# A recurrence's chunk solver on one NeuronCore: two heads or two chunks in one fp32 matmul, with orders on VectorE and ScalarE and three bulk loads moved around it

## The chip, the cores and the metric

One core of one Trainium2 chip. The metric is device time in microseconds for one execution of the whole program, as the median of several runs.

## The reference, cut to what matters

Two blocks of two layers each act on a sequence of 256 positions of 1024 features, all in fp32. Most of the work is the large products of the feed-forward layers. The change lies in one mixer, an RWKV-7 layer with 16 heads of 64 features:

```python
def step(state, inp):
    r_t, w_t, k_t, v_t, a_t, b_t = inp
    sa = jnp.einsum('bhij,bhj->bhi', state, a_t)
    state = (state * w_t[:, :, None, :] + sa[..., None] * b_t[:, :, None, :]
             + v_t[..., None] * k_t[:, :, None, :])
    y_t = jnp.einsum('bhij,bhj->bhi', state, r_t)
    return state, y_t
```

The kernel doesn't step through 256 positions. It takes chunks of 64 positions, and solves each chunk's 64 by 64 triangular system for every head by repeated doubling.

## The kernel before, in words

Weights stream from DRAM in units of 128x1024 through a ring of 6 (`RING`). ScalarE makes each unit's high part (`split_hi`), VectorE its low part (`split_lo`), up to 4 units (`AHEAD`) before TensorE uses it, and three fp32r products give fp32 accuracy. Every engine runs one fixed list of instructions; they meet at semaphores (`wait_ge`, `then_inc`).

`rwkv_in_stage` makes r, k, v and the decays. It goes through 24 units (`m` is the unit's number), with the elementwise work hung between the splits. At m = 19 and m = 21 TensorE turns tiles of them (`R.turn`, 16 transposes each), and `R.turn_out` copies the results out, even jobs on ScalarE (L1741), odd ones on VectorE (L1743). The turn at m = 19 waits for r times the decay (`R_MADE`, L2119). At its end SyncE issues the load of `g2` (L1875), and the Head's `sync` those of two rows of gains, `ln0` and `ln1` (L2612, L2614).

`solve_stage` then runs twice, for t = 0 and t = 1 (128 positions, so two chunks each), with `step_stage` behind each. It has a first part (`gram_low`, `gram_two`: products of 64x64 blocks, masked by VectorE in L2378, L2382 and L2385, while GpSimd masks in L2367), five levels (`LEVELS`), and a last part (L2303, L2308). The 16 heads are in two halves of 8 (`half`), 4 pairs (`q`) of 2 (`e`). At each level and half TensorE does

- `first_product` (L2221), called P1 here: 32 matmuls, one for each head and chunk, each with 64 rows and 64 columns of weights and 32 columns of data, so that each lies in one quadrant of the array;
- `turned` (L2228), called T: 4 transposes of 128x128;
- after both halves' P1 and T, `second_product` (L2238), called P2, of half 0 and half 1, 32 matmuls each;
- `with_values` (L2209), called V here, once a level except at the last: 32 matmuls of 64x64x64 whose results ScalarE takes out in `copy_values` (L2322).

P2 of a half waits for ScalarE's copies of P1 (L2335) and T (L2339), and for t = 0 also for VectorE's copy of one half of T (L2393). P1 of the next level waits for VectorE's addition of P2's result (`m_made`, L2400, two instructions a half, one for each `e`) and for GpSimd's mask (L2367). At levels 1 and 3 P1 of half 0 also waits for V's own end (`kv_bank`). The last part waits for the last level's `m_made`. For t = 1 the Head hangs its VectorE work in between (`while_solving`), and one long ScalarE activation (`head.square`, L2638) at level 2. 

Of the kernel before, what the change touches and what calls it, by code (L numbers as in the profile page):

```python
# [12 lines left out]
P = 128  # L13
# [185 lines left out]
def unit_done(c, eng, n):  # L199
    eng.wait_ge(c.unit_used, n + 1)  # L200
# [1597 lines left out]
def rwkv_in_stage(c, join, mu_col, recurrence):  # L1798
# [52 lines left out]
    def sync(sp):  # L1851
# [5 lines left out]
        for m in range(count):  # L1857
# [4 lines left out]
            if m == 12:  # L1862
# [10 lines left out]
                sp.dma_start(c.work[:, 19, 512:768], c.dram["smask"][:, :]).then_inc(s["rows"].sem, 16)  # L1873
        unit_done(c, sp, first + count - 1)
        sp.dma_start(c.recur[:, 3, :], c.dram["g2"][:, :]).then_inc(c.g2_in.sem, 16)  # L1875

# [170 lines left out]
    def vector(dve):  # L2047
# [15 lines left out]
        for n in range(BEFORE, AHEAD):  # L2063
            c.split_lo(dve, first + n)
        for m in range(count):
            c.split_lo(dve, first + AHEAD + m)
            if m == 0:
# [45 lines left out]
            if m == 16:  # L2113
                dve.wait_ge(*at("mix_rows", 64))
                nc.vector.scalar_tensor_tensor(wexc, kk, -1.0, wexc, ALU.mult, ALU.mult)
            if m == 17:
                unit_done(c, dve, first + 15)
                for q in range(4):
                    last = nc.vector.tensor_tensor(quad(r, q), quad(r, q), c.bank[4 + q][:, :], ALU.mult)  # L2119
                last.then_inc(s["value"].sem, 1)  # L2120
            if m == 18:
                dve.wait_ge(*at("value", R_MADE))
                nc.vector.tensor_tensor(tmp, r, k, ALU.mult).then_inc(s["value"].sem, 1)
            if m == 19:
                dve.wait_ge(*at("rows", ALL_ROWS))
                dve.wait_ge(*at("value", RK))
                order.link(dve, nc.vector.tensor_tensor(tmp, tmp, rk_row, ALU.mult))
            if m in (20, 22):
                for j in (1, 3):
                    R.turn_out(c, dve, j + 2 * (m - 20))  # L2130
            if m == 21:
# [5 lines left out]
def solve_stage(c, R, head):  # L2137
# [12 lines left out]
              "m_bank": N * LEVELS, "m_made": N * LEVELS, "final": N}  # L2150
    s = c.marks("mix_", counts)
    chunks = [slice(CHUNK * ch, CHUNK * (ch + 1)) for ch in range(2)]
    head_rows = [slice(HD * e, HD * (e + 1)) for e in range(2)]
# [63 lines left out]
    def first_product(level, half):  # L2217
        X = R.solver[half]
        for q, e, ch in quarters(((0, 0), (1, 1), (1, 0), (0, 1))):
            cols, tok = slice((2 * q + e) * CHUNK, (2 * q + e + 1) * CHUNK), chunks[ch]  # L2220
            last = nc.tensor.matmul(p_bank[half][ch][head_rows[e], q * HC:(q + 1) * HC], X.low_part[tok, cols],  # L2221
                                    right_columns(X.m[tok, cols], level), start=True, stop=True)
        last.then_inc(s["p1_bank"].sem, 1)
# [8 lines left out]
    def second_product(half):  # L2232
        X = R.solver[half]
        for q, e, ch in quarters(((0, 0), (1, 1), (0, 1), (1, 0))):
            rows, tok = head_rows[e], chunks[ch]
            left = X.t[rows, q * P + ch * CHUNK:q * P + (ch + 1) * CHUNK]
            right = X.p1[rows, ch * P + q * HC:ch * P + (q + 1) * HC]
            last = nc.tensor.matmul(m_bank[half][e][tok, q * HC:(q + 1) * HC], left, right, start=True, stop=True)  # L2238
        last.then_inc(s["m_bank"].sem, 1)
# [92 lines left out]
    def copy_products(act, level, half):  # L2332
        step, X = level * N + half, R.solver[half]
        act.wait_ge(*at("p1_bank", step + 1))
        nc.scalar.activation(X.p1[:, 0:S].rearrange("p (c n) -> p c n", c=2), p_both[half][:, :, 0:P],  # L2335
                             ACT.Copy).then_inc(s["p1_made"].sem, 1)
        act.wait_ge(*at("t_bank", step + 1))
        for i in range(1 + t):
            last = nc.scalar.activation(t_part(half, i), t_in(half, i), ACT.Copy)  # L2339
        last.then_inc(s["t_act"].sem, 1)  # L2340

    def scalar(act):
# [4 lines left out]
        for level in range(LEVELS):  # L2347
            for half in range(N):
                copy_products(act, level, half)
                if level and (level - 1) % N == half:  # L2350
                    copy_values(act, level - 1)
                if t == 1 and level == 2 and half == 0:
                    head.square(act, 0)
        for half in range(N):
# [18 lines left out]
    def vector(dve):  # L2373
# [14 lines left out]
        for level in range(LEVELS):  # L2388
# [5 lines left out]
            for half in range(N):  # L2394
                step, X = level * N + half, R.solver[half]
                dve.wait_ge(*at("m_bank", step + 1))
                for e in range(2):
                    m = pairs(X.m)[:, :, e, :].rearrange("p q (g s b) -> p q g s b", s=2, b=2 << level)[:, :, :, 1, :]
                    new = m_bank[half][e][:, 0:P].rearrange("p (q g b) -> p q g b", q=4, b=2 << level)
                    last = nc.vector.tensor_tensor(m, m, new, ALU.add)  # L2400
                last.then_inc(s["m_made"].sem, 1)
# [173 lines left out]
class Head:  # L2575
# [33 lines left out]
    def sync(self, sp):  # L2609
        c = self.c  # L2610
        sp.wait_ge(c.bonus_made.sem, c.bonus_made.at(1))
        sp.dma_start(self.ln0, c.dram["rrows"][3, :, :]).then_inc(c.g2_in.sem, 16)  # L2612
        sp.wait_ge(c.step_state.sem, c.step_state.at(2))
        sp.dma_start(self.ln1, c.dram["rrows"][4, :, :]).then_inc(self.rows.sem, 16)  # L2614

# [763 lines left out]
```

## Time and profile before

| | |
|---|---|
| median of 3 runs | 2150.77 us (2149.77 to 2151.74) |
| the profiled execution's own time | 2150.07 us |
| its span | 2148.3 us |
| TensorE, busy share of the span | 98% |
| VectorE, ScalarE, GpSimd | 71%, 53%, 17% |
| the recurrence, from the first gram product to the next stage's first product | about 1801 to 1898 us |

The span runs from the first to the last instruction of the program. Busy TensorE time contains pipelined matmuls, so it is not time at peak. A matmul's duration in the trace is its latency (0.22 us for the small ones), and several run at once; what a group costs is the distance from its start to the next group's start.

### The profile page before, as it was taken

Reading aid. Unit: us, or ns where it says so; the run is one execution under the profiler, and the core shown is the slowest. Engines: PE = TensorE matmul, PEld = TensorE weight load, DVE = VectorE, ACT = ScalarE, POOL = GpSimd, SP = SyncE. Lnnn points to the kernel's source line nnn. Section 1 sums busy time; section 2 is a strip of 40 time slices with the busy share of each in tenths; the row PEclk is TensorE's granted clock in tenths of the full one; section 3 lists DMA queues with packets and bytes.
Section 4 is the critical chain, followed back from the end, with each engine's and each line's share of the span. In section 5 each row is a group of like instructions: output and inputs, shape, how many; then the busy total and the mean of one; then the engine's idle time right before and its main releaser. Section 6 shows DMA issues by size and latency. Waiting matters only on the chain.

```text
span 2148.3 us, 39019 instructions
## 1 busy us (share of the span) xinstructions
PE 2111.2 (98%) x13570; PEld 1799.1 (84%) x13570; DVE 1515.4 (71%) x2383; ACT 1146.8 (53%) x1953; POOL 367.1 (17%) x462
## 2 busy tenths in 40 slices
PE   8999999999999999999999999999999999899998
PEld 7888888888888788888888988888888787768887
DVE  6666976667667966667667757667766797677666
ACT  5455755446446754555446446446545564355455
POOL 1111211112111211112111002111111212301111
PEclk9999999999999999999999999999999999999999
DMA  7655435555656345546556555565555452035553
GB/s 253 199 181 185 146 120 201 197 189 174 202 179 194 117 149 194 195 166 206 195 182 228 188 177 166 184 195 205 203 201 180 151 185 94 14 109 200 199 180 131
DMA packets 104401, 376.70 MB, mean 175 GB/s; under 512 B 11764, under 2 KB 12276, under 8 KB 104180
## 3 DMA queue, kind: packets, MB, share of 16 engines
q1 hardware_dynamic: 104308, 375.42, 52.2%
q8 instruction: 63, 1.03, 0.2%
q14 instruction: 30, 0.25, 0.0%
HBM read 373.29 MB, written 1.05 MB: 174 GB/s over the span
## 4 chain that ended last, share of the span: by engine, by line
PE 87%; DVE 7%; ACT 4%; issue 1%; POOL 1%; DMA 1%; SPq 0%; DVEq 0%; POOLq 0%; ACTq 0%
PE bank L951 27%; PE bank L955 14%; PE bank L190 13%; PE bank L191 13%; PE bank L192 13%; DVE w_lo L184 2%; ACT act L480 1%; PE bank L1234 1%; DVE act L591 1%; ACT w_hi L177 0%; PE bank L2238 0%; PE bank L2228 0%; PE bank L2221 0%; PE bank L390 0%; DVE x L576 0%
## 5 line engine op out<-in xcount | busy, mean ns | idle before, releaser
L951 PE MATMUL bank<-act,w_hi 128*128 128x512 f32 x2816 | 704.3, 392 | 2.6 <-DVE act L591 1.5
L951 PEld LDWEIGHTS bank<-act,w_hi 128*128 128x128 f32 x2816 | 514.7, 188 | 106.0 <-DVE act L591 4.2
L804 DVE TENSOR_TENSOR w_lo<-raw,w_hi 128x1024 fp32r<-128x1024 f32 x432 | 502.8, 1219 | 4.3 <-issue 1.0
L795 ACT ACTIVATE w_hi<-raw 128x1024 fp32r<-128x1024 f32 x432 | 424.9, 1050 | 2.3
L955 PEld LDWEIGHTS bank<-act,w_lo 128*128 128x128 f32 x2816 | 384.0, 190 | 27.7
L955 PE MATMUL bank<-act,w_lo 128*128 128x256 f32 x2816 | 392.5, 282 | 0.0
L904 DVE TENSOR_TENSOR work<-bank,work 128x256 f32<-128x256 f32 x176 | 74.7, 425 | 376.4 <-ACT work L825 376.4
L184 DVE TENSOR_TENSOR w_lo<-raw,w_hi 128x1024 fp32r<-128x1024 f32 x248 | 294.6, 1219 | 52.5 <-ACT w_hi L177 52.1
L865 POOL TENSOR_TENSOR work<-work,rb 128x256 f32<-128x256 f32 x176 | 130.0, 739 | 1035.2 <-DVE work L898 1033.5
L190 PE MATMUL bank<-w_hi,g_hi 128*128 128x512 f32 x704 | 277.3, 394 | 1.0 <-DVE w_lo L184 0.9
L191 PE MATMUL bank<-w_lo,g_hi 128*128 128x512 f32 x704 | 275.9, 392 | 0.0
L192 PE MATMUL bank<-w_hi,g_lo 128*128 128x512 f32 x704 | 274.0, 389 | 0.0
L177 ACT ACTIVATE w_hi<-raw 128x1024 fp32r<-128x1024 f32 x248 | 250.7, 1051 | 42.0 <-PE bank L192 34.8
L815 ACT ACTIVATE work<-bank 128x256 f32<-128x256 f32 x176 | 67.3, 382 | 304.7 <-PE bank L955 304.2
L820 ACT ACTIVATE work<-work 128x256 f32<-128x256 f32 x176 | 73.5, 418 | 285.2 <-POOL work L865 285.0
L190 PE MATMUL bank<-w_hi,act 128*128 128x512 f32 x496 | 197.8, 399 | 2.5 <-DVE act L2761 1.4
L192 PE MATMUL bank<-w_hi,act 128*128 128x512 f32 x496 | 193.3, 390 | 0.0
L191 PE MATMUL bank<-w_lo,act 128*128 128x512 f32 x496 | 193.3, 390 | 0.0
L192 PEld LDWEIGHTS bank<-w_hi,g_lo 128*128 128x128 f32 x704 | 132.2, 188 | 28.9
L190 PEld LDWEIGHTS bank<-w_hi,g_hi 128*128 128x128 f32 x704 | 132.8, 189 | 26.0 <-DVE w_lo L184 2.6
L191 PEld LDWEIGHTS bank<-w_lo,g_hi 128*128 128x128 f32 x704 | 132.8, 189 | 21.1
L870 POOL TENSOR_TENSOR work<-work,rb 128x256 f32<-128x256 f32 x176 | 130.2, 740 | 91.6 <-ACT work L820 91.6
(291 smaller groups left out, 2210.4 us busy)
## 6 DMA issues: line engine op xcount, KB each, us to landing
raw<-w_dram SPq DMA_DIRECT2D x680, 512.0 KB, 4.4
work<-rows_dram SPq DMA_DIRECT2D x13, 512.0 KB, 6.3
work<-rrows_dram SPq DMA_DIRECT2D x5, 512.0 KB, 4.5
x<-x_dram SPq DMA_DIRECT2D x2, 512.0 KB, 3.8
out<-x SPq DMA_DIRECT2D x4, 256.0 KB, 2.0
work<-work SPq DMA_DIRECT2D x2, 504.0 KB
work<-g_dram SPq DMA_DIRECT2D x1, 640.0 KB, 10.1
work<-dist_dram SPq DMA_DIRECT2D x2, 256.0 KB, 5.0
```

The source lines that it names most:

```text
L177: self.nc.scalar.activation(self.w_hi[:, n % RING, :], self.raw[:, n % RING, :], ACT.Copy).then_inc(self.hi_ready, 1)
L184: self.nc.vector.tensor_tensor(self.w_lo[:, n % RING, :], self.raw[:, n % RING, :], self.w_hi[:, n % RING, :].bitcast(F32), ALU.subtract). ...
L190: nc.tensor.matmul(out, stat_hi, mov_hi, start=first, stop=False)
L191: nc.tensor.matmul(out, stat_hi, mov_lo, start=False, stop=False)
L192: return nc.tensor.matmul(out, stat_lo, mov_hi, start=False, stop=last)
L795: nc.scalar.activation(c.w_hi[:, n % RING, :], c.raw[:, n % RING, :], ACT.Copy).then_inc(c.hi_ready, 1)
L804: nc.vector.tensor_tensor(c.w_lo[:, n % RING, :], c.raw[:, n % RING, :], c.w_hi[:, n % RING, :].bitcast(F32), ALU.subtract).then_inc(c.lo_ ...
L865: nc.gpsimd.tensor_tensor(c.gate_scaled[:, t % 2, :], c.gate_sum[:, t % 2, :], c.rb[:, :], ALU.mult).then_inc(s["gate_scaled"].sem, 1)
L870: nc.gpsimd.tensor_tensor(c.silu_scaled[:, t % 2, :], c.silu[:, t % 2, :], c.rb[:, :], ALU.mult).then_inc(s["silu_scaled"].sem, 1)
L904: nc.vector.tensor_tensor(c.up_sum[:, p, :], up[p][:, 0:S], c.up_sum[:, p, :], ALU.add).then_inc(s["product"].sem, 1)
L951: nc.tensor.matmul(bank[:, :], c.w_hi[:, slot(m), k * P:(k + 1) * P], c.act[:, k, :, :], start=k == 0, stop=False)
L955: return nc.tensor.matmul(bank[:, 0:S], c.w_lo[:, slot(m), k * P:(k + 1) * P], c.act_hi[:, k, :], start=False, stop=k == KT - 1)
```

## The change

P1 takes both heads of a pair as 128 columns of weights: 8 matmuls with 64 rows, 128 columns and 64 columns of data in place of 32. Half of what comes out (head e's weights with head e's data is wanted, the crossed blocks are not) is left unread. P2 takes both chunks as 128 columns of weights in the same way: 8 matmuls in place of 32. So ScalarE copies P1 out in two instructions of 64 partitions each (one for each head of the pairs), and VectorE adds P2 in four instructions a half, each over 64 partitions. `copy_values` and `head.square` come after both halves' copies of a level. In `rwkv_in_stage` VectorE's product for r comes ahead of unit 17's split, jobs 1 and 3 are copied out at m = 19 instead of 20, and the product with `rk_row` is at m = 20 instead of 19. The loads of g2 and ln0 wait for the first P1 of t = 0, that of ln1 also for the first P1 of t = 1.

```diff
@@ rwkv_in_stage, sync
-        unit_done(c, sp, first + count - 1)
-        sp.dma_start(c.recur[:, 3, :], c.dram["g2"][:, :]).then_inc(c.g2_in.sem, 16)
@@ rwkv_in_stage, vector
         for m in range(count):
+            if m == 17:
+                unit_done(c, dve, first + 15)
+                for q in range(4):
+                    last = nc.vector.tensor_tensor(quad(r, q), quad(r, q), c.bank[4 + q][:, :], ALU.mult)
+                last.then_inc(s["value"].sem, 1)
             c.split_lo(dve, first + AHEAD + m)
...
-            if m == 17:
...
             if m == 19:
+                for j in (1, 3):
+                    R.turn_out(c, dve, j)
+            if m == 20:
                 dve.wait_ge(*at("rows", ALL_ROWS))
                 dve.wait_ge(*at("value", RK))
                 order.link(dve, nc.vector.tensor_tensor(tmp, tmp, rk_row, ALU.mult))
-            if m in (20, 22):
-                for j in (1, 3):
-                    R.turn_out(c, dve, j + 2 * (m - 20))
+            if m == 22:
+                for j in (5, 7):
+                    R.turn_out(c, dve, j)
@@ solve_stage
     def first_product(level, half):
         X = R.solver[half]
-        for q, e, ch in quarters(((0, 0), (1, 1), (1, 0), (0, 1))):
-            cols, tok = slice((2 * q + e) * CHUNK, (2 * q + e + 1) * CHUNK), chunks[ch]
-            last = nc.tensor.matmul(p_bank[half][ch][head_rows[e], q * HC:(q + 1) * HC], X.low_part[tok, cols],
-                                    right_columns(X.m[tok, cols], level), start=True, stop=True)
+        for q in range(4):
+            cols = slice(q * P, (q + 1) * P)
+            for ch, tok in enumerate(chunks):
+                last = nc.tensor.matmul(p_bank[half][ch][:, q * CHUNK:(q + 1) * CHUNK], X.low_part[tok, cols],
+                                        right_columns(X.m[tok, cols], level), start=True, stop=True)
...
     def second_product(half):
         X = R.solver[half]
-        for q, e, ch in quarters(((0, 0), (1, 1), (0, 1), (1, 0))):
-            rows, tok = head_rows[e], chunks[ch]
-            left = X.t[rows, q * P + ch * CHUNK:q * P + (ch + 1) * CHUNK]
-            right = X.p1[rows, ch * P + q * HC:ch * P + (q + 1) * HC]
-            last = nc.tensor.matmul(m_bank[half][e][tok, q * HC:(q + 1) * HC], left, right, start=True, stop=True)
+        for q in range(4):
+            for e, rows in enumerate(head_rows):
+                right = X.p1[rows, 0:S].rearrange("p (c q n) -> p c q n", c=2, n=HC)[:, :, q, :]
+                last = nc.tensor.matmul(m_bank[half][e][:, q * CHUNK:(q + 1) * CHUNK], X.t[rows, q * P:(q + 1) * P],
+                                        right, start=True, stop=True)
...
     def copy_products(act, level, half):
-        nc.scalar.activation(X.p1[:, 0:S].rearrange("p (c n) -> p c n", c=2), p_both[half][:, :, 0:P],
-                             ACT.Copy).then_inc(s["p1_made"].sem, 1)
+        for e, rows in enumerate(head_rows):
+            own = p_both[half][rows, :, 0:S].rearrange("p c (q e n) -> p c q e n", e=2, n=HC)[:, :, :, e, :]
+            last = nc.scalar.activation(X.p1[rows, 0:S].rearrange("p (c q n) -> p c q n", c=2, n=HC), own, ACT.Copy)
+        last.then_inc(s["p1_made"].sem, 1)
...
             for half in range(N):
                 copy_products(act, level, half)
-                if level and (level - 1) % N == half:
-                    copy_values(act, level - 1)
-                if t == 1 and level == 2 and half == 0:
-                    head.square(act, 0)
+            if level:
+                copy_values(act, level - 1)
+            if t == 1 and level == 2:
+                head.square(act, 0)
...
                 for e in range(2):
-                    new = m_bank[half][e][:, 0:P].rearrange("p (q g b) -> p q g b", q=4, b=2 << level)
-                    last = nc.vector.tensor_tensor(m, m, new, ALU.add)
+                    new = m_bank[half][e][:, 0:S].rearrange("p (q c g b) -> p q c g b", q=4, c=2, b=2 << level)
+                    for ch, tok in enumerate(chunks):
+                        last = nc.vector.tensor_tensor(m[tok], m[tok], new[tok, :, ch, :, :], ALU.add)
@@ Head.sync
+        grams_over = [recurrence.first_product for recurrence in self.R]
+        sp.wait_ge(grams_over[0].sem, grams_over[0].at(1))
+        sp.dma_start(c.recur[:, 3, :], c.dram["g2"][:, :]).then_inc(c.g2_in.sem, 16)
         sp.wait_ge(c.bonus_made.sem, c.bonus_made.at(1))
         sp.dma_start(self.ln0, c.dram["rrows"][3, :, :]).then_inc(c.g2_in.sem, 16)
         sp.wait_ge(c.step_state.sem, c.step_state.at(2))
+        sp.wait_ge(grams_over[1].sem, grams_over[1].at(1))
         sp.dma_start(self.ln1, c.dram["rrows"][4, :, :]).then_inc(self.rows.sem, 16)
```

On VectorE, from the split of unit 17 to the end of `rwkv_in_stage`, the order before (L184 is a split, L2119 the product for r, L2123 r times k, L2127 the product with `rk_row`, L1743 a copy of turned tiles, L2132 the sum for the bonus):

```order
L2115 SCALAR_TENSOR_TENSOR work<-work 128x2048
L184 TENSOR_TENSOR w_lo<-raw,w_hi 128x1024
L2119 TENSOR_TENSOR work<-work,bank 128x512 x4
L184 TENSOR_TENSOR w_lo<-raw,w_hi 128x1024
L2123 TENSOR_TENSOR work<-work 128x2048
L184 TENSOR_TENSOR w_lo<-raw,w_hi 128x1024
L2127 TENSOR_TENSOR work<-work 128x2048
L184 TENSOR_TENSOR w_lo<-raw,w_hi 128x1024
L1743 COPY recur<-bank 128x512 x2
```

and of the change (L2118 is the old L2115, L2067 the old L2119, L2121 the old L2123, L2128 the old L2127):

```order
L2118 SCALAR_TENSOR_TENSOR work<-work 128x2048
L2067 TENSOR_TENSOR work<-work,bank 128x512 x4
L184 TENSOR_TENSOR w_lo<-raw,w_hi 128x1024 x2
L2121 TENSOR_TENSOR work<-work 128x2048
L184 TENSOR_TENSOR w_lo<-raw,w_hi 128x1024
L1743 COPY recur<-bank 128x512 x2
L184 TENSOR_TENSOR w_lo<-raw,w_hi 128x1024
L2128 TENSOR_TENSOR work<-work 128x2048
```

The product for r is one split earlier, and the first two copies come before the product with `rk_row`; the copies of jobs 5 and 7 keep their place.

On ScalarE, levels 1 and 2 of the solver for t = 1, before (L2335 copies P1, L2339 T, L2322 V's result, L2638 is the Head's square):

```order
L2335 ACTIVATE work<-bank 128x256
L2339 ACTIVATE work<-bank 128x2x128 x2
L2322 ACTIVATE work<-bank 128x512
L2335 ACTIVATE work<-bank 128x256
L2339 ACTIVATE work<-bank 128x2x128 x2
L2335 ACTIVATE work<-bank 128x256
L2339 ACTIVATE work<-bank 128x2x128 x2
L2638 ACTIVATE recur<-work 128x1024
L2335 ACTIVATE work<-bank 128x256
L2339 ACTIVATE work<-bank 128x2x128 x2
L2322 ACTIVATE work<-bank 128x512
```

and of the change (L2340, L2344, L2325 and L2648 in their places):

```order
L2340 ACTIVATE work<-bank 64x256 x2
L2344 ACTIVATE work<-bank 128x2x128 x2
L2340 ACTIVATE work<-bank 64x256 x2
L2344 ACTIVATE work<-bank 128x2x128 x2
L2325 ACTIVATE work<-bank 128x512
L2340 ACTIVATE work<-bank 64x256 x2
L2344 ACTIVATE work<-bank 128x2x128 x2
L2340 ACTIVATE work<-bank 64x256 x2
L2344 ACTIVATE work<-bank 128x2x128 x2
L2325 ACTIVATE work<-bank 128x512
L2648 ACTIVATE recur<-work 128x1024
```

The copies of half 1 no longer stand behind V's copy or the square.

## Rows read from the trace of the kernel before

**Rows 1.** The page's first part: busy time, share of the span, instructions.
```profile
PE 2111.2 (98%) x13570; PEld 1799.1 (84%) x13570; DVE 1515.4 (71%) x2383; ACT 1146.8 (53%) x1953; POOL 367.1 (17%) x462
```
**Rows 2.** Window, t = 1's levels: length; busy PE, PEld, DVE, ACT, POOL; clock; DMA; GB/s.
```profile
1857.00:1880.00 23.00, 19.90 (x703) 17.13 (x701) 14.45 (x27) 10.78 (x29) 12.91 (x7) 1.00 0.02 4
```
**Rows 3.** Timeline of TensorE, two other stages: start us, length us, line, weights, data, count.
```profile
283.92 1.05 PE L1249 MATMUL bank<-const,work 128*128 128x1 f32 x8
...
247.90 1.14 PE L1200 MATMUL bank<-work 64*128 64x256 f32 x8
```
**Rows 4.** Groups by line and shape, P1: count, busy us, mean ns, idle before.
```profile
L2221 PE MATMUL bank<-work 64*64 64x32 f32 x640 | 15.1, 221 | 3.0 <-issue 1.5 <-DVE work L2382 0.9
```
**Rows 5.** Timeline of TensorE, levels 1 to 4 of t = 0, to the last part's first matmul.
```profile
1812.31 1.04 PE L2221 MATMUL bank<-work 64*64 64x32 f32 x32
...
1822.06 0.67 PE L2221 MATMUL bank<-work 64*64 64x32 f32 x32
...
1823.24 0.67 PE L2221 MATMUL bank<-work 64*64 64x32 f32 x32
1823.84 0.66 PE L2228 MATMUL bank<-const,work 128*128 128x128 f32 x4
1824.43 1.35 PE L2238 MATMUL bank<-work 64*64 64x32 f32 x64
1825.57 1.10 PE L2209 MATMUL bank<-work 64*64 64x64 f32 x30
1826.45 0.25 PE L2221 MATMUL bank<-work 64*64 64x32 f32 x2
...
1830.72 0.69 PE L2303 MATMUL bank<-work 64*64 64x64 f32 x32
```
**Rows 6.** VectorE and ScalarE: copies of T in both solvers, an addition of P2's result.
```profile
1824.54 0.42 DVE L2393 COPY work<-bank 128x256 f32<-128x256 f32 x1 [0.76 <-PE bank L2228]
1830.09 0.48 DVE L2400 TENSOR_TENSOR work<-work,bank 128x128 f32<-128x128 f32 x2 [0.20 <-PE bank L2238]
...
1877.43 0.66 ACT L2339 ACTIVATE work<-bank 128x256 f32<-128x256 f32 x2 [0.17 <-PE bank L2228]
```
**Rows 7.** Timeline of TensorE, t = 1, with the idle time ahead in brackets.
```profile
1848.37 2.30 PE L2196 MATMUL bank<-recur 64*64 64x128 f32 x75 [0.95 <-issue]
...
1857.65 0.30 PE L2221 MATMUL bank<-work 64*64 64x32 f32 x4
...
1876.13 0.67 PE L2221 MATMUL bank<-work 64*64 64x32 f32 x32
...
1878.23 1.06 PE L2238 MATMUL bank<-work 64*64 64x32 f32 x32 [0.24 <-ACT work L2339]
1879.11 0.69 PE L2303 MATMUL bank<-work 64*64 64x64 f32 x32
...
1882.55 0.27 PE L2308 MATMUL bank<-work 64*64 64x64 f32 x2 [0.54 <-issue]
```
**Rows 8.** Waits from 1800 to 1900 us: in total, times, longest.
```profile
PE bank L2238 <- ACT work L2339: 1.7, 5, 0.6
...
PE bank L2221 <- issue: 1.5, 4, 0.5
```
**Rows 9.** Timelines at the head: TensorE's turn and first gram product, VectorE's last copies.
```profile
1785.46 1.94 PE L1731 MATMUL bank<-const,work 128*128 128x128 f32 x16 [1.05 <-DVE work L2119]
...
1800.87 0.69 PE L2189 MATMUL bank<-recur 64*64 64x64 f32 x32
...
1798.82 1.28 DVE L1743 COPY recur<-bank 128x512 f32<-128x512 f32 x2
```
**Rows 10.** VectorE's mask L2382 for t = 0 and t = 1, and GpSimd's two masks beside it.
```profile
1803.83 0.69 DVE L2382 TENSOR_TENSOR work<-work,const 128x512 f32<-128x512 f32 x1
...
1847.73 1.69 DVE L2382 TENSOR_TENSOR work<-work,const 128x512 f32<-128x512 f32 x1
...
1802.69 2.97 POOL L2367 TENSOR_TENSOR work<-work,const 128x512 f32<-128x512 f32 x2 [30.34 <-ACT work L2315]
```

More of the change, by code:

```diff
@@ L2115, in vector @@
                 nc.vector.scalar_tensor_tensor(wexc, kk, -1.0, wexc, ALU.mult, ALU.mult)
-            if m == 17:
[L2117 to L2120, printed above, removed]
             if m == 18:
@@ L2151, in solve_stage @@
     s = c.marks("mix_", counts)
+    R.first_product = s["p1_bank"]
     chunks = [slice(CHUNK * ch, CHUNK * (ch + 1)) for ch in range(2)]
```

## The prediction

> **What bounds the kernel.** I read the page first: TensorE is busy 98% of the span [rows 1], so outside the recurrence the kernel is a stream of matmuls that this change leaves alone. What can move lies between about 1782 and 1898 us. Next I read the window of t = 1's levels: the granted clock is 1.00 (2.4 GHz), no engine but TensorE is near full, and even TensorE has only 19.9 us busy in 23 [rows 2]. Then the timeline of TensorE through the levels, group by group [rows 5, 7], because busy time of overlapping small matmuls says little; the waits tell what ended its gaps [rows 8]. The reader should see a chain there: P1 and T of half 0, P1 and T of half 1, copies of T, P2 of half 1, V, next level. TensorE waits for ScalarE 5 times, 1.7 us in all, and P1's matmuls alone were held back 1.5 us by "issue", that is by no semaphore [rows 8]; these sit inside groups and are waits for instructions, as I read them.
>
> **P1 and P2 on TensorE.** Today P1 has 32 matmuls in 0.60 us from its start to T's (1823.24 to 1823.84) [rows 5], 8 in each quadrant. A P1 matmul lasts 221 ns [rows 4], so some 0.38 of the 0.60 us is issue and the rest is the end of the last one, which T needs since it uses the whole array. In the change 8 matmuls lie in two row groups, 4 in each. What do 4 cost? With 128 columns of weights and a single column of data the pitch is (1.05 - 0.25) / 7 = 0.114 us (L1249) [rows 3], so such a matmul is paced by its weights, and 64 columns of data hide behind them. Two row groups run side by side: 8 matmuls of 64x128 with 256 columns take 1.14 us, where one after another would be twice that (L1200) [rows 3]. So 4 x 0.114, less what the first doesn't wait for, is 0.40 us to the last start, and 0.15 for its end: 0.55 us. **A quarter of the matmuls, but 0.05 us less for a group.** A P2 goes the same way: 0.40 in place of the 0.57 that the pair's 1.14 us give it (1824.43 to 1825.57) [rows 5]. But V behind it works in 64x64, and P1 behind V in 64x128. I charge 0.14 us for each such change of shape, as P1 to T has it (0.15 above), so P2 of half 1 to V is 0.54 and V to P1 is 0.88 + 0.13 = 1.01 us (1825.57 to 1826.45) [rows 5], or about 1.27 where P1 waits for V's end (levels 1 and 3; 1.24 today).
>
> No row here has 64x64 next to 64x128, so nothing may be lost there; that is the lower end, 12 x 0.13 = 1.6 us better. The Trainium skill, TensorEngine Tiling (Array Packing), Key Properties, says that changing the tiling mode drains TensorE, which speaks for the charge and against the change. By that rule my sum stands; without it the sum would be 1.6 us lower.
>
> **The chain through the copies.** Let y be the start of half 1's P1. T of half 1 starts at y + 0.55. In t = 0 VectorE's copy starts 0.70 after T does and takes 0.42 (1823.84, 1824.54) [rows 5, 6], and P2 starts 0.12 later: y + 1.79 in place of y + 1.84. In t = 1 ScalarE has two copies, 0.66, starting 0.70 after T, and P2 follows at 1878.23, 0.14 after 1878.09 [rows 6, 7]: y + 2.05 in place of the 2.10 of level 4 (1876.13 to 1878.23). The second copy of P1 costs ScalarE 0.28 us more (0.66 for two against 0.385 for one), and hides: P1's copies start at y + 0.70 and leave the engine free at y + 1.26, when T is there. So faster matmuls alone bring 0.05 us a half.
>
> **The longer addition.** Two additions take 0.48 us (1830.09) [rows 6], so the pitch is 0.20 and four take 0.89. They bear on the path once in each solver, at its end: the last part's first matmul waits for half 0's addition. That was 1.36 after P2's start, and becomes 0.70 + 0.89 + 0.15 = 1.74. Elsewhere half 0's addition ends by y + 2.87, while V keeps TensorE until y + 3.3, and that cover is 0.45 us in t = 0 and 0.7 in t = 1. The 64 partitions I take at the price of 128.
>
> **Sum for t = 0**, levels 1 to 4: the blocks are 0.55 + 0.58 + 1.79 + 0.54 + 1.01 = 4.47; with the wait 4.73; 4.47; and last 0.55 + 0.58 + 1.14 + 1.74 = 4.01. That is 17.7 against 1830.72 - 1812.31 = 18.4 [rows 5]: **-0.7 us**, all of it from stalls such as that of level 1's P1, which takes 1.04 in place of 0.67. Level 0 doesn't change.
>
> **Sum for t = 1**: 0.55 + 0.58 + 2.05 + 0.54 + 1.01 = 4.73; 4.99; 4.73; 4.01; in all 18.5 against 1879.11 - 1857.65 = 21.5 [rows 7]: -3.0, less 0.1 at level 0: **-2.9 us**. Two things make it: 1.45 us of P1's stalls go (1920 of TensorE's instructions fewer in the two solvers, a matmul and a load of weights for each of 960), and half 1's copies no longer stand behind copy_values and the square, of the 1.7 us of waits the larger part. The square moved by 2 us still ends before VectorE has added half 1 of level 2 and asks for it.
>
> **The loads.** g2 and ln0 (1 MB) land during t = 0's first levels instead of its gram products, ln1 5 us later than before. Their readers come much later (gain row and gate in t = 1), so the delay costs nothing. With ln1 away from t = 1's gram products I expect the stall of 0.95 us there [rows 7] to go. But VectorE is the longer there, its L2382 taking 1.69 us [rows 10], so TensorE's gain is hidden, but for an earlier P1: GpSimd's next mask is then out of the way of VectorE's second L2382. **-0.4**, between 0 and -0.6. The stall of 0.54 in the last part [rows 7] should go with the others, as the queue is ahead: **-0.4**.
>
> **VectorE in rwkv_in_stage.** The turn at m = 19 waits 1.05 us for the product for r [rows 9]; a split earlier it is there 1.1 us sooner, and TensorE reaches the gram product at 1799.8 or sooner. But job 7 must be out first, and VectorE, which is full here with the same work in another order, copies it until 1800.10 [rows 9]. So the gram starts at 1800.2 in place of 1800.87: -0.7. Against it: GpSimd's masks come 1 us sooner with ScalarE, VectorE's first L2382 0.7 us sooner. In t = 0 it slipped between GpSimd's two masks (0.69), in t = 1 it met the second one and took 1.69 [rows 10]. I expect t = 0 to meet it too, +1.0, and half of that back at the second L2382. **-0.2**, between -0.7 and +0.3.
>
> **Sum**: -0.2 - 0.7 - 0.4 - 2.9 - 0.4 = -4.6 us, from the profiled execution's 2150.07 (span 2148.3) to 2145.5. The median of the runs is 0.7 above that execution, so the forecast is **2146.2**. A measurement of this kernel tells about 0.2%, 4.3 us, from no change; the forecast is just past it.
>
> **The rivals.**
> *Instructions go on stalling* (chance 0.22). The stalls may follow the fetching of blocks and not how many instructions are used, or come back elsewhere. For it: V and the gram products, as dense as before, remain, and the bulk loads now lie beside the levels. Against it: t = 0's gram products ran without a stall beside a bulk load. Then about 1.45 + 0.7 + 0.4 of the gain is lost, nearly 2.7 with the hidden 0.1: 2148.9.
> *No charge for a change of shape* (0.17): 1.6 us lower, 2144.6.
> *The matmuls are paced by their number* (0.04). At 0.60 / 32 = 19 ns each, 8 would take 0.15. That shortens each P1 and P2 by a further 0.25 on the path, three groups in each of 8 levels, 6 us: 2140. L1249's pitch speaks against it.
> *Slower: the clock falls* (0.03). The granted clock is 1.00 with TensorE 87% busy [rows 2]; the change issues a quarter of the P1 and P2 matmuls. If that took the clock to 1.2 GHz in the levels of t = 1, groups worth about 3.5 us a level would double, 4 x 3.5 = 14 us: 2160. It decides from the first window where the clock reads under 1; two levels of it outweigh the gain. Nothing in the rows is near it.
> *VectorE and GpSimd meet badly in both solvers*, or the added copies don't hide (0.04): 1.5 to 2 us lost, 2148.
>
> **The numbers.** My forecast has 0.50, and of its spread of about 1 us 0.6 lies past 0.2%. Faster: 0.30 + 0.17 + 0.04 = 0.51. Within 0.2%: 0.20 + 0.22 + 0.04 = 0.46. Slower 0.03. The range reaches from the second rival less 1 us to the first plus 0.6 us: 2143.5 to 2149.5.
>
> **What would show it.** P1 to T 0.55 us with 8 matmuls; P2 of half 1 to V 0.54; in t = 1 P2 of half 1 at P1 + 2.05 in each level; levels of 4.5 us in t = 0 and 4.8 in t = 1; no "issue" gap over 0.2 us in the solvers; the first gram product at 1800.2; the addition 0.89. A P1 group under 0.4 us, a V that follows P2 at once, or gaps by "issue" of the old size would each prove a step wrong.

## The result, and the profile after

The change takes 2161.57 us (2161.27 to 2162.39), the kernel before, beside it on the same chip, 2151.26 us (2149.77 to 2153.04). The ratio is 1.0051, with an interval of 1.004 to 1.0061: **slower by 10.3 us**. The forecast was 2146.2, its range ended at 2149.5, and slower by over 0.2% had a chance of 0.03. The profiled execution took 2161.52 us, its span 2159.7.

The page's first part, which answers to [rows 1]:

```profile
PE 2128.1 (99%) x12930; PEld 1816.4 (84%) x12930; DVE 1531.4 (71%) x2423; ACT 1155.1 (53%) x1973; POOL 366.9 (17%) x462
```

TensorE has 640 matmuls fewer than before, 13570 less 12930. The prediction took 960. The groups by line and shape, 1780 to 1912 us, show why (count, busy us, mean ns, idle before); P1 is L2224, P2 L2240:

```profile
L2224 PE MATMUL bank<-work 64*128 64x64 f32 x320 | 22.2, 277 | 0.8 <-PE bank L2211 0.6
L2240 PE MATMUL bank<-work 64*128 64x64 f32 x320 | 21.0, 276 | 0.1
```

In 20 groups (5 levels, 2 halves, 2 solvers) 320 is 16 a group, not 8. **One fp32 matmul call of the code is two matmuls in the trace**, and two loads of weights. Before, P1 calls 16 matmuls a group (4 pairs, 2 heads, 2 chunks) and the trace has 32; the change calls 8 and the trace has 16. The text ahead set the code's 8 beside the trace's 32. The number is halved, not quartered.

The timeline of TensorE through level 2 of t = 0, where before has [rows 5], and the end of the levels (start, length, line, weights, data, count, idle time before in brackets):

```profile
1819.35 1.11 PE L2224 MATMUL bank<-work 64*128 64x64 f32 x16
1820.39 0.66 PE L2231 MATMUL bank<-const,work 128*128 128x128 f32 x4
1820.98 1.11 PE L2224 MATMUL bank<-work 64*128 64x64 f32 x16
...
1822.61 2.00 PE L2240 MATMUL bank<-work 64*128 64x64 f32 x32
1824.54 1.15 PE L2211 MATMUL bank<-work 64*64 64x64 f32 x32
1825.85 1.11 PE L2224 MATMUL bank<-work 64*128 64x64 f32 x16 [0.16 <-PE bank L2211]
...
1835.36 2.00 PE L2240 MATMUL bank<-work 64*128 64x64 f32 x32
1837.84 0.69 PE L2306 MATMUL bank<-work 64*64 64x64 f32 x32 [0.48 <-DVE work L2406]
```

P1 to T is 1.04 us (1819.35 to 1820.39), 0.60 before and 0.55 predicted. The two P2 take 1.93 to V (1822.61 to 1824.54), 1.14 before. The level is made of TensorE alone: twice P1 to T (1.04) and T to the next group (0.59), the two P2 (1.93) and V to P1 (1.31) are 6.50 us; 0.16 of it is a wait for V's end. Before, levels 1 to 3 of t = 0 took 4.7 us each on average, from P1's start to the next P1's.

The starts of the single matmuls in the same trace say how they lie. In the change's P1 they start in pairs, the two of a pair 7 ns apart, and behind the first pair a new one starts every 0.112 us. Before, P1's start in fours, again 7 ns apart, and behind the first four new ones start every 0.058 us. So two matmuls with 128 columns of weights lie side by side, and four with 64 columns do.

Windows of the levels of t = 0 and t = 1 (length; busy PE, PEld, DVE, ACT, POOL; clock; DMA; GB/s):

```profile
1812.00:1831.00 19.00, 18.68 (x312) 16.81 (x308) 9.18 (x30) 8.31 (x21) 7.64 (x6) 1.00 0.01 2
1857.00:1880.00 23.00, 22.38 (x340) 19.35 (x337) 19.25 (x38) 11.17 (x29) 10.20 (x7) 1.00 0.08 25
```

In t = 1 TensorE is busy 22.4 us of 23 with 340 matmuls, against 19.9 with 703 in [rows 2]. Neither ScalarE nor VectorE holds it up for long: in t = 1 a level takes 6.49 us where the same level of t = 0 takes 6.26, because the second half's P2 starts some 0.2 us later, behind ScalarE's copies: the two P2 take 2.16 us to V there (1874.60 to 1876.76), in place of 1.93. The granted clock is 1.00 in both: it isn't the cause.

Two more lines, of TensorE at the first gram product and at the last part of t = 1, and of VectorE:

```profile
1799.85 0.69 PE L2191 MATMUL bank<-recur 64*64 64x64 f32 x32 [1.31 <-DVE recur L1743]
...
1894.21 0.27 PE L2311 MATMUL bank<-work 64*64 64x64 f32 x2 [1.02 <-issue]
```
```profile
1802.80 1.69 DVE L2387 TENSOR_TENSOR work<-work,const 128x512 f32<-128x512 f32 x1
...
1836.51 2.39 DVE L2406 TENSOR_TENSOR work<-work,bank 64x128 f32<-64x128 f32 x8 [0.62 <-PE bank L2240]
```

Where the time went, start of the change less start of before: the gram product of t = 0 comes 1.0 us earlier (1799.85, 1800.87), the last part of t = 0 7.1 us later (1837.84, 1830.72), the last part of t = 1 11.2 later (1890.30, 1879.11). The stage behind and the end of the span have 11.4 to 11.7. So 8.1 us are lost between the first gram product and the last part of t = 0, 4.1 between there and the last part of t = 1, and 0.5 in the last part's longer stall (1.02 in place of 0.54). Nearly all of it is in the two solvers' levels: levels 1 to 4 take 24.7 and 25.5 us, where before has 18.4 and 21.5.

### The profile page after: what moved, and what is told of

It is laid out like the page before. It is cut to its first block, busy times and chain, and to the rows that moved or that the text cites. A ratio compares the mean times of both kernels' runs of the same rounds, so it can differ in the third digit from the quotient of the medians.

```text
span 2159.7 us, 37800 instructions
## 1 busy us (share of the span) xinstructions
PE 2128.1 (99%) x12930; PEld 1816.4 (84%) x12930; DVE 1531.4 (71%) x2423; ACT 1155.1 (53%) x1973; POOL 366.9 (17%) x462
## 4 chain that ended last, share of the span: by engine, by line
PE 87%; DVE 7%; ACT 3%; issue 2%; POOL 1%; DMA 1%; SPq 0%; DVEq 0%; POOLq 0%; ACTq 0%
PE bank L951 27%; PE bank L955 14%; PE bank L190 13%; PE bank L191 12%; PE bank L192 12%; DVE w_lo L184 2%; PE bank L2224 1%; PE bank L2240 1%; ACT act L480 1%; PE bank L1234 1%; ACT w_hi L177 1%; DVE act L591 1%; PE bank L2231 0%; PE bank L390 0%; DVE x L576 0%
## 5 line engine op out<-in xcount | busy, mean ns | idle before, releaser
L184 DVE TENSOR_TENSOR w_lo<-raw,w_hi 128x1024 fp32r<-128x1024 f32 x248 | 294.6, 1220 | 52.0 <-ACT w_hi L177 51.6
```

The lines of the kernel that those rows point to most:

```text
L184: self.nc.vector.tensor_tensor(self.w_lo[:, n % RING, :], self.raw[:, n % RING, :], self.w_hi[:, n % RING, :].bitcast(F32), ALU.subtract). ...
```

## The experiments

The theory after the result: **pairs load 128 columns for each matmul and lie in two row groups, so half the matmuls take longer than all of them in four quadrants.** Rivals: the copies and additions over 64 partitions; the new orders and loads. Each time below stands beside a kernel before of its own, measured along with it, and the ratio is to that one; those of the runs below lie between 2150.8 and 2152.1 us.

**a1: the orders and loads without the new products.** P1, P2, their copies and additions are those of before.

```diff
-                last = nc.tensor.matmul(p_bank[half][ch][:, q * CHUNK:(q + 1) * CHUNK], X.low_part[tok, cols], ...
+            last = nc.tensor.matmul(p_bank[half][ch][head_rows[e], q * HC:(q + 1) * HC], X.low_part[tok, cols], ...
```

> The change without its new products: P1 and P2, their copies and additions as before; only the orders on VectorE and ScalarE and the three moved loads remain. If the new groups of TensorE are what costs (P1 start to T 1.04 us after, 0.60 before), this is faster than before: the gram product starts about 1 us sooner, half 1's P2 in t = 1 loses its waits behind V's copy and the square (about 1 us), so 2147 to 2150 us. If the orders or the loads are what costs, it is as slow as the change, 2158 us or more.

2151.85 us, ratio 0.9999 (0.999 to 1.0009). That misses the 2147 to 2150, and it is nowhere near 2158. Taken together the orders and loads bring nothing and cost nothing; the loss is in the products and what hangs on them. In a1's trace the two solvers differ. In t = 1, with ScalarE's new order, levels 1 to 4 take 20.0 us, before 21.5. In t = 0 they take 21.7, before 18.4. There the gain goes into a stall and the half clock behind it, as TensorE's timeline and a window of a1 show:

```profile
1826.84 0.64 PE L2223 MATMUL bank<-work 64*64 64x32 f32 x28
1828.89 0.30 PE L2223 MATMUL bank<-work 64*64 64x32 f32 x2 [1.42 <-issue]
```
```profile
1830.00:1837.00 7.00, 7.00 (x199) 6.60 (x194) 2.32 (x7) 2.11 (x6) 0.00 (x0) 0.52 0.02 5
```

Inside a P1, TensorE waited 1.42 us for nothing that the profile shows; 1 us later the granted clock was at half (1.2 GHz) for 6.8 us. That is one execution, a slow one among a1's ten (2152.97 us).

**a2: the same results in quadrants.** The banks, the split copies and the additions are the change's; P1 and P2 go back to one head and one chunk a matmul.

```diff
-        for q in range(4):
-            cols = slice(q * P, (q + 1) * P)
-            for ch, tok in enumerate(chunks):
-                last = nc.tensor.matmul(p_bank[half][ch][:, ...], X.low_part[tok, cols], ...
+        for q, e, ch in quarters(((0, 0), (1, 1), (1, 0), (0, 1))):
+            last = nc.tensor.matmul(p_bank[half][ch][head_rows[e], ...], X.low_part[tok, own], ...
```

> The change with its wide products cut into quadrants: each matmul has 64 columns of weights and 64 of data, the same results in the same places, twice the number of matmuls, and the split copies and additions stay. Theory 'weights' (a matmul with 128 columns of weights is paced by loading them, 0.111 us each, and only two run side by side): P1 to T goes back to 0.60 us though the number of matmuls doubles and each still moves 64 columns, levels to 4.5 to 5 us, time 2147 to 2152. Rival 'splits' (two copies and four additions are what costs): P1 may shorten but the time stays above 2157. Rival 'data' (64 columns of data in place of 32 are what costs): P1 stays near 1.0 us.

2154.58 us, ratio 1.0013 (1.0004 to 1.0023). Its TensorE:

```profile
1817.93 0.69 PE L2223 MATMUL bank<-work 64*64 64x64 f32 x32
1818.55 0.66 PE L2230 MATMUL bank<-const,work 128*128 128x128 f32 x4
```

P1 has 32 matmuls with the change's 64 columns of data and takes 0.62 us to T, against 1.04. Against its own before a2 is 2.8 us slower where the change is 10.3, so with the same results in the same places 7.5 us are gone. The time misses the 2147 to 2152 as well as the rival's 2157. What stays lies in t = 1: its levels 1 to 4 take 23.8 us, where a1 has 20.0, and TensorE waits there 2.3 us in five for ScalarE's copies and 1.4 us once for an addition. The theory holds for the larger part, and the rival has a share in this narrow solver.

**a3: P1 with half the columns of data.**

```diff
-                                        right_columns(X.m[tok, cols], level), start=True, stop=True)
+                                        right_columns(X.m[tok, q * P:q * P + CHUNK], level), start=True, stop=True)
...
```

> The change with P1's data cut to 32 columns (the first head's of each pair, used for both heads, so the solution is wrong for half of the heads; the count of matmuls and copies stays). Theory 'weights': P1 to T stays at 1.04 us, pitch 0.111 us for each row group, and the time stays that of the change within 1 us. Rival 'data': P1 falls to 0.6 to 0.8 us.

2161.11 us, from a single run. A P1 in it:

```profile
1819.54 1.08 PE L2224 MATMUL bank<-work 64*128 64x32 f32 x16
1820.55 0.66 PE L2231 MATMUL bank<-const,work 128*128 128x128 f32 x4
```

Half the data takes 0.03 us off 1.04, and the pairs of matmuls still start every 0.112 us. In a2, with 64 columns of weights and the same 64 of data as the change, the fours start every 0.058. The crossed blocks cost next to nothing; the matmuls are paced by their weights, as the prediction had it.

**a4: the splits alone.** Before, with P1 copied out in two instructions and P2 added in four. ScalarE keeps its old order, with V's copy and the square ahead of half 1's copies.

```diff
-                    last = nc.vector.tensor_tensor(m, m, new, ALU.add)
+                    for tok in chunks:
+                        last = nc.vector.tensor_tensor(m[tok], m[tok], new[tok], ALU.add)
...
```

> The kernel before with only the copies of P1 cut into two instructions of 64 partitions and the additions into four. Theory 'weights': the copies hide and the additions cost 0.4 us at the end of each solver: 0 to 1.5 us slower than before. Rival 'splits': 5 us slower or more.

2155.06 us, ratio 1.0016 (1.0006 to 1.0025), 3.2 us slower than its before and about twice the most that was expected. Its window of t = 1, two lines of its VectorE, and what its P2 waited for in 1800 to 1912 (total, times, longest), against 1.7 us in 5 of [rows 8]:

```profile
1860.00:1885.00 25.00, 19.74 (x696) 17.07 (x690) 23.89 (x45) 13.73 (x37) 12.33 (x7) 1.00 0.01 3
```
```profile
1872.91 2.39 DVE L2403 TENSOR_TENSOR work<-work,bank 64x128 f32<-64x128 f32 x8
...
1883.64 1.18 DVE L2403 TENSOR_TENSOR work<-work,bank 64x128 f32<-64x128 f32 x4
```
```profile
PE bank L2238 <- ACT work L2341: 5.3, 8, 1.5
```

An addition over 64 partitions takes 0.30 us, where 0.20 was reckoned, and with the Head's work VectorE is nearly full in t = 1: 23.9 us of 25. But what TensorE waits for is mostly ScalarE: 5.3 us in eight for the copies of T behind P1's two copies, which with V's copy and the square ahead of them don't hide. So a4 prices the split copies in ScalarE's old order, which the change has not, more than the additions. Its trace is also of the slowest of its ten executions (2156.83 us), with a stall of 1.21 us in t = 0 and 6.8 us of half clock behind it.

**b1 and b4: V between the two P2**, in a1 and in before, to fill the wait for the copies.

```diff
+            if half == 0 and level < LEVELS - 1:
+                if level % N == 1:
+                    pe.wait_ge(*at("p1_made", step + 2))
+                with_values(pe, level)
```

> As the run of the orders alone (P1 and P2 as before, orders and loads of the change), but V stands between P2 of half 0 and P2 of half 1, so that TensorE works while half 1's copies are made and P1 at levels 1 and 3 need not wait for V's end. If the chain of copies and these waits are what is left on the path in the narrow solver, each block of a level gets 0.2 to 0.5 us shorter, 2 to 3 us in all against the orders alone: 2148 to 2150. If instruction supply bounds the solver (stalls by issue), the gaps come back elsewhere and the time stays at 2151 to 2153.

> The kernel before with only V moved between the two P2 of a level. By the chain of copies: 1 to 3 us faster than before, 2149 to 2151. By instruction supply: the same as before.

b1: 2150.56 us, ratio 1.0000 (0.999 to 1.0009), between its two ranges. b4: 2150.32 us, 0.9998 (0.9988 to 1.0007), the same as before. The waits for ScalarE's copies go (1.2 us in a1) and stalls come instead. The waits of b1, of TensorE in 1800 to 1912 (total, times, longest), against 1.5 us in 4 of [rows 8]:

```profile
PE bank L2223 <- issue: 4.7, 5, 1.3
```

**b2: a1 with the loads in their old places; b3: before with VectorE's new order alone.**

```diff
+        unit_done(c, sp, first + count - 1)
+        sp.dma_start(c.recur[:, 3, :], c.dram["g2"][:, :]).then_inc(c.g2_in.sem, 16)
```

> The orders alone, with the three loads where they were before. Theory 'moved loads cost': g2 and ln0 beside the levels of t = 0 delay the instructions, and the stall of 1.4 us at level 4 of t = 0 and the half clock behind it go away here: about 2148.5 to 2150. Rival 'the stall comes by chance of where blocks of instructions fall': the stall is there with the old loads too, or another in its place, and the time is that of the orders alone within 1 us.

> The kernel before with only VectorE's order in rwkv_in_stage changed. The first gram product starts 1.0 to 1.2 us sooner (1799.7), TensorE waits 1.3 us for job 7's copy ahead of it. If that reaches the end, 2149.8 to 2151 beside a before of 2151.8; if VectorE's mask L2382 now meets GpSimd's, the solver's first P1 is no sooner and the time that of before.

b2: 2150.94 us, ratio 1.0002 (0.9993 to 1.0012). b3: 2151.86 us, 1.0006 (0.9996 to 1.0016): its gram product comes 1.4 us earlier (1799.47), and none of that reaches the end. TensorE's gram products of b3 and of b2:

```profile
1804.75 1.64 PE L2199 MATMUL bank<-recur 64*64 64x128 f32 x51 [1.83 <-issue]
```
```profile
1805.73 2.72 PE L2200 MATMUL bank<-recur 64*64 64x128 f32 x51 [1.92 <-issue]
```

With the new order and the loads in their old places the gram products of t = 0 stall 1.8 to 1.9 us; before and a1 have no such stall there. So the moved loads do spare that stall, but no time comes of it: a1, with them moved, is no faster than b2. The stall of a1 at level 4 is in b2 too (1.42 us): the moved loads don't make it.

**c1 and c2: only P1, or only P2, with pairs.**

```diff
-        for q, e, ch in quarters(((0, 0), (1, 1), (1, 0), (0, 1))):
+        for q in range(4):
+            for ch, tok in enumerate(chunks):
```

> The change with P2 and its additions as before, so P1 alone is wide. By the pace of the weights P1 to T is 1.04 us against 0.60, 16 groups of it bear on the path beside the fewer stalls: 2154 to 2158 us, about half of the change's loss. If the loss is in P2 or in the additions, 2150 to 2152.

> The change with P1 and its copies as before, so P2 alone is wide, with four additions a half. By the pace of the weights the two P2 take 1.93 us to V against 1.14, and V to P1 is 0.15 longer for the change of shape: 2154 to 2158 us. If the loss is in P1 or its copies, 2150 to 2152.

c1: 2154.55 us, ratio 1.0018 (1.0008 to 1.0027). c2: 2154.24 us, 1.0016 (1.0007 to 1.0026). Each alone costs 3.5 to 3.8 us, about a third of the whole. Both lie within their ranges, though c1's "about half" was too much. Each comes with its own split copies or additions. Level 2 of t = 0 in c2:

```profile
1818.47 0.67 PE L2223 MATMUL bank<-work 64*64 64x32 f32 x32
1819.66 2.00 PE L2239 MATMUL bank<-work 64*128 64x64 f32 x32
1821.59 1.15 PE L2211 MATMUL bank<-work 64*64 64x64 f32 x32
```

P2 has its 1.93 us with P1 narrow: the price belongs to the shape, not to the pair of changes.

**c3: does the number of instructions bind the narrow solver?** b1 with V in half as many matmuls of twice the data; every second head's weights are left out of V.

```diff
-        for j in range(8):
+        for j in range(0, 8, 2):
```

> The run with V between the two P2, with V in half as many matmuls of twice the columns of data: the same time on TensorE for V (0.9 us), 32 instructions fewer of some 336 a level; every second head's weights are left out of V, so the output is wrong there. Theory 'the narrow solver is bound by how fast its instructions arrive' (256 in some 3.6 us, a level of 336 in 4.75): levels get 0.3 to 0.45 us shorter, stalls by issue fall by as much, 2 to 3 us in all against that run: 2147.5 to 2149. Rival 'the stalls don't depend on how many instructions there are': same levels, 2150 to 2151.

2146.63 us, ratio 0.9981 (0.9972 to 0.9991), 4 us less than b1 and just past the range. Its waits:

```profile
PE bank L2223 <- issue: 1.8, 4, 0.6
```

P1, which was not touched, stalls 1.8 us in place of 4.7, and V takes the same 0.9 us. Fewer instructions do help the narrow solver, as the prediction argued. How they help is less plain: all of TensorE's gaps by "issue" fall by 1.6 us only, from 6.7 to 5.1. In b1's trace the granted clock is also at half for 3.4 us twice, once 1.7 us behind a stall of 1.25; c3's has no such stretch. Of the instruction queue's packets in 1812 to 1830 us (packets, MB, share of 16 engines' time), before and the change:

```profile
q8 instruction: 5, 0.08, 1.8%
```
```profile
q8 instruction: 2, 0.03, 0.7%
```

b1 and c3 have 5 packets each there, so this view doesn't tell those two apart.

**d1: the count that the prediction reckoned with.** The whole change, with P1 and P2 in half as many matmuls of twice the data. The weights of 2 of the 4 pairs are used on the data of all 4.

```diff
-        for q in range(4):
+        for q in range(0, 4, 2):
...
-                last = nc.tensor.matmul(p_bank[half][ch][:, q * CHUNK:(q + 1) * CHUNK], X.low_part[tok, cols],
-                                        right_columns(X.m[tok, cols], level), start=True, stop=True)
+                last = nc.tensor.matmul(p_bank[half][ch][:, q * CHUNK:(q + 2) * CHUNK], X.low_part[tok, cols],
+                                        right_columns(X.m[tok, q * P:(q + 2) * P], level), start=True, stop=True)
```

> The whole change, with P1 and P2 of every half made in half as many matmuls, each of twice the data columns (weights of 2 of the 4 pairs on the data of 4, so the products of two pairs are with another pair's weights). The copies, the additions, T, V, the waits and the orders stay. A group of P1 then has 8 matmuls in the trace, 4 in each row group, which is the number that the prediction reckoned with. If the count was the step that failed and its pitch was right: P1 to T 0.55 to 0.60 us (1.04 in the change), both P2 to V about 1.05 (1.93), levels of t = 0 about 4.6 to 4.9 us (6.25 to 6.5), 1.5 to 1.8 us less in each of 8 levels, so 2147 to 2150. Rival: the loss sits in what stays, the copies and additions over 64 partitions and the changes of shape between V, P1 and T: the levels then get less than 0.8 us shorter each and the time stays at 2155 or more.

2152.38 us, ratio 1.0005 (0.9996 to 1.0014). Each against its own before, the forecast was 4.6 us faster, the change is 10.3 slower and d1 0.3 slower: of the 14.9 us between forecast and result 10.0 are gone, and 4.9 are not. It missed its 2147 to 2150 and the rival's 2155. TensorE in level 2 of t = 0, and at level 3 of t = 1:

```profile
1816.77 0.71 PE L2224 MATMUL bank<-work 64*128 64x128 f32 x8
1817.42 0.66 PE L2231 MATMUL bank<-const,work 128*128 128x128 f32 x4
1818.00 0.72 PE L2224 MATMUL bank<-work 64*128 64x128 f32 x8
...
1819.23 1.52 PE L2240 MATMUL bank<-work 64*128 64x128 f32 x16
1820.69 1.15 PE L2211 MATMUL bank<-work 64*64 64x64 f32 x32
1821.99 0.71 PE L2224 MATMUL bank<-work 64*128 64x128 f32 x8 [0.16 <-PE bank L2211]
...
1870.36 0.72 PE L2224 MATMUL bank<-work 64*128 64x128 f32 x8 [1.21 <-DVE work L2406]
```

P1 to T is 0.65 us with 8 matmuls (0.55 predicted); the pairs start every 0.112 us here too, now with 128 columns of data. Levels 1 to 4 of t = 0 take 19.8 us (1811.78 to 1831.54) against 24.7 in the change and 17.7 predicted. In t = 1 they take 23.0, against 25.5 and 18.5. There VectorE is nearly full, and TensorE waits 1.2 us for it at level 3 (above) and in five places, 2.2 us in all, for ScalarE's copies of T (window 1857 to 1880; one such P2; the waits in 1800 to 1912):

```profile
1857.00:1880.00 23.00, 19.11 (x281) 15.35 (x276) 22.12 (x41) 13.57 (x37) 12.31 (x7) 1.00 0.01 2
```
```profile
1867.36 0.72 PE L2240 MATMUL bank<-work 64*128 64x128 f32 x8 [0.50 <-ACT work L2344]
```
```profile
PE bank L2240 <- ACT work L2344: 2.2, 5, 0.5
```

This P2 starts 2.44 us after its half's P1 (1864.92), where the prediction had 2.05.

## Why the prediction was wrong

**The step that failed** is "In the change 8 matmuls lie in two row groups, 4 in each. What do 4 cost?". There are 16, 8 in each. By the prediction's own working, 8 x 0.114 less 0.06 for the first, plus 0.15, is 1.01 us, and P1 takes 1.04. Two P2 are 16 x 0.114 less 0.06, plus 0.14, or 1.91, and they take 1.93. The pitch (0.112 measured), the two row groups side by side, and weights as what paces them were right (a2, a3, the starts of single matmuls). The same trace held the contradiction: [rows 4] has 640 for a loop that calls 16 a group, and the order of the code's instructions counts calls. Against the 0.60 and 1.14 of before, a level takes 2 x 0.44 + 0.79 = 1.67 us more of TensorE's time, where it was to take less. With 16 and 32 in place of 8 and 16, the prediction's own sum gives about 24.0 us for levels 1 to 4 of each solver (an estimate, from its other terms as they stand). It had 17.7 and 18.5, and the trace has 24.7 and 25.5. So the count is some 11.8 of the 14.0 us missed there. Level 0, which was not to change, takes 1.3 and 1.0 us longer from its P1 to the next. d1, which has the count that was reckoned with, is 10.0 us faster than the change; that is not the same quantity, since its matmuls have twice the data and its waits differ.

Why pairs lose then: before, P1's 32 matmuls are in four quadrants, 8 in each, one every 0.058 us. One with 128 columns of weights takes twice that, 0.112, and only two lie side by side. Half the matmuls, at twice the time, with half as many at once, are twice the time: 0.89 us against 0.45, without the end of the last.

**The smaller mis-sized terms** are the split copies and additions.
- "The second copy of P1 costs ScalarE 0.28 us more (0.66 for two against 0.385 for one), and hides". Two took 0.77 us, not 0.66. In d1 they don't hide in t = 1: half 1's P2 comes 2.44 us after its P1, not 2.05, in four levels. In the change, where TensorE is slower, they hold that P2 up by some 0.2.
- "The 64 partitions I take at the price of 128". Four additions took 1.18 us, not 0.89. From the last P2 to the last part it is 2.48 us (1835.36 to 1837.84), predicted 1.74; of these 0.74 us, 0.29 are the additions and 0.45 are the count again, since the first addition waits for a longer P2.
- The rival "or the added copies don't hide", with its 0.04, is what a4 shows for ScalarE's old order and what part of d1's 4.9 us are. The prediction read VectorE at 14.5 us of 23 from [rows 2]; with four additions a half it is busy 22.1 us of 23 in d1 and 23.9 of 25 in a4, and in d1 TensorE waits 1.2 us for it once.

**What stood.**
- A change of shape costs something. V to the first P1 is 1.07 us (1818.28 to 1819.35), predicted 1.01, where before, with all of it 64x64, has 0.88 [rows 5]: so 0.19 rather than the 0.13 charged. The last matmul of a wide P1 is also 0.20 us ahead of T, where a narrow one is 0.15. The Trainium skill, TensorEngine Tiling (Array Packing), Key Properties, says that changing the tiling mode drains TensorE. By that rule, V to P1 had to get longer, and the trace agrees.
- P1's stalls by "issue" go: gaps of TensorE over 0.15 us by "issue" in 1800 to 1912 fall from 3.6 us in 7 to 1.0 in 1. The rival that they go on is wrong for this kernel; in a1 and b1, which keep the narrow products, they do go on. Whether the smaller number of instructions or the slower pace at which TensorE now uses them did it, no run separates.
- The gram stall of 0.95 us in t = 1 is gone. The last part's of 0.54 is not: it is 1.02 now.
- The first gram product came at 1799.85, predicted 1800.2, and VectorE's first L2382 (now L2387) took 1.69 us. By P2 of level 0 nothing is left of the head's gain: 1809.86 against 1809.87. Predicted was 0.2. The first mask ate it whole, and the second, 1.10 us against 1.08, gave nothing back.
- The clock stayed at 1.00 in the levels. It fell to half for 3.4 us at 1910.2, behind them, and the distance to before is 11.7 us on both sides of that.

So part of the mechanism was there: with fewer instructions P1's stalls of 1.5 us and the gram product's of 0.95 went, as forecast. That the last part's grew by 0.5 was not. The price of the wider weights was halved by a count, and the verdict turned on that.

How the parts add up stays open in part. P1 and P2 alone cost 3.8 and 3.5 us with their own splits, together 7.3 of the 10.3; the 3.2 of a4 are no third part as they stand, since its trace has 3.6 us more of waits for ScalarE than before, and the change's P2 shows no idle time for them. Open too is what a wide solver with additions over 128 partitions would take; it wasn't tried.

## What to carry to other kernels

Count instructions in one currency: take the number from the trace's rows of before, divide by the calls in the code, and carry that factor to the new code. Weigh packing by what one matmul loads and how many lie side by side: here, with 32 to 64 columns of data, 64x64 in four quadrants beat 64x128 in two row groups, though it took twice the instructions. An engine's room is to be read in the stretch where it has the most other work, with the new instruction's price measured at its own shape. And a wait names the engine: a4's VectorE was the fuller one, but TensorE waited for ScalarE.

## What the runs showed of the hardware

- A matmul call in fp32 is two matmuls and two loads in the trace: 16 calls, 32 rows.
- fp32 matmuls with 128 columns of weights over 64 rows started two at a time every 0.112 us, with 32, 64 or 128 columns of data (a3, the change, d1). With 64 columns of weights they started four at a time every 0.058 us, with 32 or 64 columns of data (before, a2).
- An addition of 128 elements a partition lasts 0.28 to 0.29 us, over 128 partitions or over 64. Two over 128 partitions start 0.20 us apart, so they overlap. Those over 64 partitions start 0.30 apart and don't, in a4 too, where the access pattern is that of before. P1's copies on ScalarE do the same: 0.38 us each over 64 or 128 partitions, and 0.77 for the two halves, where two copies of T over 128 partitions take 0.66. Why the halves don't overlap, no run shows.
- Seven stalls by "issue" of 1.2 to 1.9 us came inside dense small matmuls. Behind four of them (a1 1.42, a4 1.21, b1 1.25, b2 1.92) the granted clock fell to half within 0.4 to 1.8 us, for 3.4 to 6.8 us. Behind three (b1 1.22, b2 1.42, b3 1.83) it did not. So the length of the stall alone doesn't decide it.
- The stalls move: taking away waits (b1 against a1) raised TensorE's gaps by "issue" from 4.3 us to 6.7, and taking away instructions (c3) lowered them to 5.1.
